# A weight unit is split three units ahead of TensorE instead of two

## The reference

```
# first block
h = rms_norm(x, g_mix);  q,k,v,z,f,scal,gates = split(h @ w_in)
y_a = gated_deltanet(conv+silu(q,k,v), z, scal, ...) @ w_dn_up   # two directions, chunks of 64,
                                                                 # triangular solve, scan of 4 chunks
y_f = real(fft2(f)) @ w_fourier
x = x + (gate_a * y_a + gate_f * y_f) @ w_o
h = rms_norm(x, g_mlp);  x = x + square(relu(h @ w_mlp_up)) @ w_mlp_down
x = rms_norm(x, g_final)
# second block
proj = rms_norm(x, pre_g) @ w_in_2   # a_u a_v a_g b_x b_g x_q x_g gates
y_a = a_u * (causal(w_s) @ layer_norm(a_v) + b_s) * silu(a_g)
y_b = s5(b_x, complex states of 64 groups x 64) -> gelu -> glu, * silu(b_g)
y_x = cross_attention(x_q, rms_norm(mem) @ xa_wk, ... @ xa_wv) * silu(x_g)
out = x + rms_norm((sum_n sigmoid(gates_n) * (y_n @ w_branch_n)) @ w_out, post_g)
```

## Time and profile before

| | before |
|---|---|
| median of 3 runs | 2296.23 us |
| profiled execution, its own time | 2300.16 us |
| its span | 2298.4 us |
| mean granted TensorE clock | 0.994 |
| TensorE busy | 2258.7 us, 98% |
| weight loads of TensorE | 1957.5 us, 85% |
| VectorE (DVE) busy | 1762.1 us, 77% |
| ScalarE (ACT) busy | 1027.1 us, 45% |
| GpSimd (POOL) busy | 298.0 us, 13% |
| chain that ended last: PE, DVE | 84%, 11% |

### The profile page before, as it was taken

How to read it: one execution, slowest core, us unless ns; L and a number is a source line. 1 busy time by engine, 2 the same in 40 slices (tenths; PEclk the granted TensorE clock), 3 DMA queues, 4 the chain that set the end, 5 groups by cost and what they waited for, 6 DMA issues and landing times.

```text
span 2298.4 us, 30093 instructions
## 1 busy us (share of the span) xinstructions
PE 2258.7 (98%) x12660; PEld 1957.5 (85%) x12660; DVE 1762.1 (77%) x1974; ACT 1027.1 (45%) x850; POOL 298.0 (13%) x226
## 2 busy tenths in 40 slices
PE   8999999999999999999999999899999999999998
PEld 7988888888888888888888888788888888888886
DVE  7595568657797898787766889979999968458865
ACT  5553335334444545445444435344444444544432
POOL 0002200210000000000000000045887500000000
PEclk9999999999999999999999999999999999999999
DMA  7443454347755555555555566566666687576754
GB/s 271 147 159 138 147 200 153 140 147 258 276 201 201 202 201 220 202 203 202 205 205 206 204 222 227 185 244 214 210 210 212 210 294 256 192 243 250 264 205 146
DMA packets 84230, 475.19 MB, mean 207 GB/s; under 512 B 8704, under 2 KB 8832, under 8 KB 32512
## 3 DMA queue, kind: packets, MB, share of 16 engines
q1 hardware_dynamic: 84096, 473.27, 58.1%
HBM read 450.17 MB, written 23.07 MB: 206 GB/s over the span
## 4 chain that ended last, share of the span: by engine, by line
PE 84%; DVE 11%; DMA 2%; issue 1%; ACT 1%; DVEq 0%; SPq 0%; ACTq 0%
PE acc L2180 26%; PE acc L2183 25%; PE acc L2186 25%; DVE w_lo L1263 4%; PE banks L2327 2%; PE banks L2376 1%; DMA raw<-in_w 1%; DVE a_raw L1310 1%; DVE convT L1583 1%; DVE padT L1310 1%; PE banks L2455 1%; ACT w_hi L803 1%; DMA spilled<-stage 1%; PE banks L2197 1%; DVE stats L1377 0%
## 5 line engine op out<-in xcount | busy, mean ns | idle before, releaser
L1263 DVE TENSOR_TENSOR w_lo<-raw,w_hi 128x2048 fp32r<-128x2048 f32 x394 | 912.4, 2318 | 352.7 <-ACT w_hi L803 349.7
L803 ACT ACTIVATE w_hi<-raw 128x2048 fp32r<-128x2048 f32 x394 | 751.2, 1912 | 630.8 <-DMA raw<-in_w 630.2
L2180 PE MATMUL acc<-w_hi,a_hi 128*128 128x512 f32 x2112 | 815.1, 386 | 14.5 <-DVE w_lo L1263 9.4
L2183 PE MATMUL acc<-w_lo,a_hi 128*128 128x512 f32 x2112 | 802.7, 380 | 0.0
L2186 PE MATMUL acc<-w_hi,a_lo 128*128 128x512 f32 x2112 | 802.2, 380 | 0.0
L2180 PEld LDWEIGHTS acc<-w_hi,a_hi 128*128 128x128 f32 x2112 | 400.3, 190 | 84.7 <-issue 13.4
L2186 PEld LDWEIGHTS acc<-w_hi,a_lo 128*128 128x128 f32 x2112 | 400.4, 190 | 57.5 <-DVE a_lo L1299 0.3
L2183 PEld LDWEIGHTS acc<-w_lo,a_hi 128*128 128x128 f32 x2112 | 400.5, 190 | 54.0
L2180 PE MATMUL acc<-w_hi,b_hi 128*128 128x512 f32 x928 | 352.3, 380 | 0.0
L2183 PE MATMUL acc<-w_lo,b_hi 128*128 128x512 f32 x928 | 351.7, 379 | 0.0
L2186 PE MATMUL acc<-w_hi,b_lo 128*128 128x512 f32 x928 | 351.7, 379 | 0.0
(11 more groups left out here) (351 smaller groups left out, 1680.6 us busy)
## 6 DMA issues: line engine op xcount, KB each, us to landing
raw<-in_w SPq DMA_DIRECT2D x395, 1024.0 KB, 4.8
spilled<-stage SPq DMA_DIRECT2D x72, 256.0 KB, 5.9
gate_in<-spilled SPq DMA_DIRECT2D x20, 512.0 KB, 5.8
x_rows<-in_x SPq DMA_DIRECT2D x4, 512.0 KB, 9.1
x_rows<-in_x SPq DMA_DIRECT2D x1, 2048.0 KB, 10.3
mem_rows<-in_mem SPq DMA_DIRECT2D x2, 1024.0 KB, 5.9
spilled<-stage_b SPq DMA_DIRECT2D x8, 256.0 KB, 5.8
out<-y_rows SPq DMA_DIRECT2D x3, 512.0 KB, 2.8
```

The source lines that it names most:

```text
L803: act.activation(w_hi[:, n % HIGH, :], raw[:, n % RAW, :], ACT.Copy)\
L1263: dve.tensor_tensor(w_lo[:, n % RAW, :], raw[:, n % RAW, :], w_hi[:, n % HIGH, :].bitcast(F32), ALU.subtract).then_inc(lo_split, 1)
L2180: pe.matmul(o, hi[:, tk], wh, start=first, stop=False)
L2183: pe.matmul(o, hi[:, tk], wl, start=False, stop=False)
```

## The change

`AHEAD` goes from 2 to 3. On ACT and on DVE slot n now holds the split of unit n+3, at the same position in the slot. Slot 0 issues two splits, of units 2 and 3, one behind the other; later slots issue one; the last three slots none.

```diff
-AHEAD = 2
+AHEAD = 3
 EARLY = 2
@@ ACT, and the same on DVE
             def slot_work(n):
                 run_steps(me, steps, 2 * n)
-                if n + AHEAD < UNITS:
-                    split(n + AHEAD)
+                for m in range(EARLY if n == 0 else n + AHEAD, min(n + AHEAD + 1, UNITS)):
+                    split(m)
```

## The result

The changed kernel took 2325.49 us (median of 4 runs, 2323.95 to 2326.97), the kernel before 2295.86 us beside it (4 runs, 2295.29 to 2297.37). The ratio is 1.0129, 95% interval 1.0113 to 1.0145: slower by 29.6 us. I had forecast slower by 15.3 us, 2311.5; the measured time lies 1.5 us outside my range. The profiled execution took 2326.97 us, its span is 2325.2 us and the mean granted clock 0.991, for 0.994 before.

What follows compares the result with a forecast made beforehand. The prediction took TensorE, busy 98%, as the bound. Its terms, 3.1 + 0 + 4.3 + 4.0 - 7.4 + 6.2 + 5.1 = +15.3 us, on a median of 2296.2 gave 2311.5 us, range 2293 to 2324.

Steps and rivals of the forecast that it cites:

- signs of being wrong: Stalls at heads, norm or 2159 us below 1.5 us, or the state space set-up giving less than 5 us.
- The rival that the room of the steps covers the delay: Whole kernel: stalls go and the steps' room covers the delay, -23.7 us, 2272.5; chance 0.12, partial case included.
- heads: 549 to 572 us: one more split ahead on DVE delays heads and the last `a_lo`, +4.3 us.
- norm: Gating's layer norm, 1870 to 1896 us: statistics stand behind unit 324's split, gating matmuls start late, +6.2 us.
- last branch: 2159 us: DVE has no idle time, one more `w_lo` delays the four `a_lo`, +5.1 us with clock.
- the one that the split hardly moves: Whole kernel: ACT is held by the landing, gains and losses about 7 us each way, 2296; chance 0.12.
- The one with +1 us at each delta step: Two delta chains, 31 steps each: delay returns at half of each, 1 us each, +30 more, 2342; chance 0.06.
- Start: First units: `a_lo` behind the splits of units 3 and 4 delay units 2 and 3, +3.1 us.
- Delta rule: I take 0.: 130 to 420 us: four `w_lo` stalls go, but next results come unready; 0, ends -5 and +5.
- Smaller places: +4.0.: y_in +1.1, fourth piece of mlp +0.8, first hidden +0.7, first operand of w_branch2 at 2117 us +1.4.
- State space set-up: -7.4.: 1440 to 1485 us: stalls of 5.3 and 2.4 us go, DVE's groups come behind their splits, -7.4 us.
- the clock's rule in the prediction: TensorE: a new stall of 2.4 us or more costs 1.7 us of clock, one under 1.8 nothing.

Runs made afterwards that it cites:

- ACT alone: Kernel before with splits three units ahead on ACT only, DVE staying at two: 2294.0 us, ratio 0.9990.
- half step: Kernel before with the split of unit n+3 at the end of slot n on ACT and DVE, passing only even-place steps: 2301.03 us, ratio 1.0024.
- delta piece: Kernel before with ACT and DVE three units ahead only in slots 14 to 59, the delta rule: 2300.07 us, ratio 1.0018.
- the piece alone: Kernel before with ACT and DVE three units ahead only in slots 243 to 256, the state space set-up: 2291.11 us, ratio 0.9982.
- start: Kernel before with ACT and DVE three units ahead only in slots 0 to 13: 2299.80 us, ratio 1.0019.
- fill: Kernel before with growing chains of small DVE additions ahead of the splits of eight units, 150 to 220: 2315.93 us in one run.
- heads: Kernel before with ACT and DVE three units ahead only in slots 70 to 79: 2301.36 us, ratio 1.0024.
- mlp: Kernel before with ACT and DVE three units ahead only in slots 84 to 241 (y_in, mlp, memory): 2301.89 us, ratio 1.0025.
- last: Kernel before with ACT and DVE three units ahead only from slot 257 on (gating's norm, last branches): 2309.90 us, ratio 1.0066.
- spread version: Kernel before, both engines two ahead, with some small DVE operations and products of the state space set-up moved later: 2290.29 us, ratio 0.9976.

## Why the prediction was right in sign and wrong in size

**The bound and the mechanism: right.** TensorE is busy 98%, the stalls on `w_lo` are what can go, ACT is held by the landing; ACT's wait for landings stayed above 500 us, as said. One of my signs of being wrong was met by a little: the state space set-up gave 4.8 us timed alone (5.3 by the two traces), and I had asked for 5. That a loss is a step behind a split in DVE's queue is shown by ACT alone and by the half step. The rival that the room of the steps covers the delay (2272.5) fell at heads, norm and the last branch; the one that the split hardly moves (2296) fell with the waits of 344 places. The one with +1 us at each delta step (2342) fell too: the delta piece cost 4.1.

**Start, heads, norm, last branch: right in place and nearly in size.** 3.1, 4.3 and 12.7 (with 2117) were forecast, 4.0, 5.4 and 14.1 measured. At heads the stall came to 4.85 us, not 3.9 at most: the first product ended at 555.88, 548.6 on the old clock, 1.1 us later than my 547.5, because the `w_lo` ahead of it waited 2.85 us for ACT's half. The sum of the start holds though its second stall didn't come: the half clock filled its room. Norm came out within 0.4 us partly by luck. I had unit 325 3.4 us late and the clock's loss hidden in the second wait; it was 1.5 us late, because the statistics took 3.2 us (1898.22 to 1901.40) where I had carried over 5.0 (last section), and the half clock came behind the second wait, at 1914.9, and cost its 1.7 us.

**The steps that failed** are three terms of the sum:

- "Delta rule: I take 0." Measured +4.1. I had seen the squares, convT and the first solve level as what comes next, and then let my layout, good to 0.6 us, cancel them against the stalls that go. It left out that a stall of 2.2 to 2.3 us there can also take the clock: in the changed kernel the stretches at 191.2, 358.4 and 396.0 us, 1.7 us each, against one that went. That is 3.4 of the 4.4 us by which TensorE falls back there in the two traces. How the timed +4.1 divides isn't shown, since the clock fell otherwise in the piece's own trace.
- "Smaller places: +4.0." Without 2117 I had 2.6; measured +5.6. The fourth piece of mlp was +0.8 and is +4.3 in the trace: 2.4 us of stall and 1.7 of clock. Before, x_rows ended at 702.82 and TensorE came to it at 705.32, 2.5 us of room; in the changed kernel it ended at 722.47, 707.8 on the old clock, so 5.0 us later and not the 3.3 that my 0.8 implies. The clock's 1.7 us wasn't in the term at all.
- "State space set-up: -7.4." Measured -4.8. My layout let units 248 and 249 wait 0.7 us each; unit 248 waited 4.24. The first group was laid out as if DVE had caught up before it. In the piece alone unit 248 waited 2.37 us, so of the 4.24 the layout itself missed about 1.7 us, and 1.9 go with the deeper splits ahead of slot 243, which I had at nothing. Against that, unit 252 waited 1.47 us and not 2.8: the group of 7.9 us ahead of its split holds a copy that took 1.86 us before and 0.17 in the changed kernel (last section). Before, DVE is busy 30.8 of 34 and 23.1 of 25 us there (the windows below, columns as in the earlier trace rows), and the idle rest is a wait of 1.65 us for ACT and waits on its own results; so one unit of lead turns the stall at unit 247 into a shorter one a unit later.

```profile
1427.00:1461.00 34.00, 28.73 (x120) 24.35 (x119) 30.80 (x58) 15.81 (x18) 0.00 (x0) 0.90 0.54 172
1461.00:1486.00 25.00, 22.60 (x97) 19.19 (x96) 23.10 (x48) 8.84 (x7) 1.80 (x1) 0.93 0.60 211
```

These three make 9.7 of the 13.1 us between 15.3 and 28.4; the other 3.4 are the sum of small misses of the same sign. A part of all is the clock's rule in the prediction, 1.7 us for stalls of 2.4 us or more: it said nothing of stalls between 1.8 and 2.4 us, and in the changed kernel four stalls of 2.21 to 2.37 us took it as well, 6.8 us that stand nowhere in my sum.

**The way from span to median** cost 2.8 us more. The profiled execution of before stood 4 us above its median, that of the changed kernel 1.5. Before's took up unit 0 at 9.39 us, 1.4 us later than the changed kernel's (7.97), by two waits in the preparation of x (5.32 and 2.11 us, for 4.80 and 1.19) that differ in the traces of all these kernels; it had half clock for 6.8 us after the set-up's stall, where two of the nine other traces with a stall of over 5 us there (start and fill) have 3.4. Its stretch at 94.9 us, which follows no long stall, explains nothing here, since the changed kernel's trace has it too, at 99.0. I subtracted the 4 us from a forecast whose own execution need not have them.

**The range** was too narrow because its upper end took +5 for the delta rule, +5 for the smaller places and 2.3 us at heads and norm together, and no error of the clock's count; and the lower end had all clock losses absent, which none of the runs bears out.

**A rule beside it.** The order of each queue was kept: in the earlier trace rows and after, no step passed a waiting split. The Trainium skill (TensorE: Matmul & The Clock Gate, Architectural detail) says so of ACT and DVE, and the trace agrees: 462.9 us of waiting on DVE, and the stall on heads behind one of them. The Trainium skill's advice to speed what TensorE waits for (Perfetto Trace Analysis, Optimization Strategies) gave 2.3 us where it was done on ACT alone, and cost 29.6 where it was done on DVE too.

## What to carry to other kernels

Moving a prefetch step forward in an engine's in-order queue pays only as far as that engine is idle ahead of the stall; otherwise the stall changes its name and is found at the first result that TensorE takes at once. Judge such a move place by place, apply it per engine and per place, and where a busy group stands in one piece, spread the group instead. In a sum of stalls, a new one of 2 us or more is priced with the half clock that may follow it, 1.7 us here, and a stall that is forecast to shrink below that size is not.

## What the runs showed of the hardware that I had not expected

The granted clock fell to half behind stalls from 1.56 us on in some traces and stayed full behind stalls up to 2.42 us in others; behind 2.50 us or more it always fell, the first 10 us of a trace apart. It fell for 3.4 or for 6.8 us after the same stall of 5.3 us in different executions, and in the delta rule's piece for 6.8 us behind one of 2.16 us and not at all behind one of 2.41. Seven of the 16 traces also have 3.4 us of half clock near 95 us (94.3 to 99.0), with no stall of 0.6 us or more in the 40 us before it. So one trace is uncertain by 1.7 us or more at each such place, which is as much as most of the terms that it is read for.

Some small operations of DVE lasted until an instruction of GpSimd (POOL) that ran beside them was over. Before, the copy at line 1840 (128 x 32 values) took 1.86 us, 1463.29 to 1465.15, beside a POOL memset from 1463.31 to 1465.11, and the small product at line 1389 took 1.99 us beside a POOL product that ended 0.02 us ahead of it. In the changed kernel POOL wasn't at work at either time, and each took 0.17 us. The copy took 0.62 to 1.83 us in five of the pieces (delta rule, heads, mlp, start, last), each time until 0.03 to 0.05 us after the memset's end; the 0.19 us operations with two operands that ran beside the same memset in the spread version weren't lengthened. So the durations that I carried over from before held a neighbour's work: 1.8 us at norm and 1.7 at the set-up.
